# Query projection of a hybrid trunk layer: head groups A and B in three chunks of 512 columns instead of four of 384

## The reference, cut to what matters

```python
z = h @ w_in                                   # h: (384, 2048), w_in: (2048, 3648)
a_q, a_k, a_v, b_q, b_k, b_v, c_q, c_ckv, c_kr = jnp.split(z, PROJ_SPLITS, axis=-1)
q_a = apply_rope(rms_norm(a_q, lp["a_qn"]), *rope_hd)      # latent tiles; context tiles without the rope
q_b = apply_rope(rms_norm(b_q, lp["b_qn"]), *rope_hd)
...                                            # attention of each group
mix = merge_heads(o_a, o_b, o_c) @ w_o
x = x + g1 * mix
x = x + g2 * hier_moe(modulate(rms_norm(x, g_ffn), sh2, sc2))   # 32 experts of 512, top 2
```

## Time and profile before

| | us |
|---|---|
| median of 3 runs | 1730.23 (1730.15 to 1730.38) |
| the profiled execution's own time | 1730.17 |
| its span, first to last instruction | 1728.3 |
| TensorE busy, matmuls | 1619.3 (94% of the span) |
| VectorE / ScalarE / GpSimd busy | 619.3 / 265.4 / 99.0 |
| read from HBM | 584.04 MB |

### The profile page before, as it was taken

One profiled execution on the slowest core, in us unless ns is written; L12 is line 12 of the kernel. 1 busy time (PEld: TensorE's weight loads), 2 busy tenths in 40 slices (PEclk: granted clock), 3 DMA queues, 4 the chain that ended last, 5 costly groups with the idle time before them and its releaser, 6 DMA issues.

```text
span 1728.3 us, 18419 instructions
## 1 busy us (share of the span) xinstructions
PE 1619.3 (94%) x6799; PEld 661.0 (38%) x6844; DVE 619.3 (36%) x1333; ACT 265.4 (15%) x709; POOL 99.0 (6%) x189
## 2 busy tenths in 40 slices
PE   5999999999989999999999999999899989988998
PEld 2445545544433444444323332332333233233332
DVE  3112222102226201352443454444444443544444
ACT  2003221102224100011011101101110110111010
POOL 1022100101011100000000000000000000000000
PEclk8999999999999999999999999999999999999999
DMA  9994671755569722189999999999999999999995
GB/s 369 384 342 195 250 270 62 281 211 205 227 225 374 316 97 97 60 331 425 425 429 427 427 429 426 425 428 424 425 428 425 428 425 427 426 426 427 416 428 223
DMA packets 92639, 581.93 MB, mean 337 GB/s; under 512 B 9110, under 2 KB 24310, under 8 KB 55390
## 3 DMA queue, kind: packets, MB, share of 16 engines
q1 hardware_dynamic: 84944, 554.20, 78.9%
q0 software_dynamic: 5920, 22.61, 3.5%
q10 hardware_dynamic: 1728, 4.51, 0.7%
HBM read 584.04 MB, written 7.05 MB: 342 GB/s over the span
## 4 chain that ended last, share of the span: by engine, by line
PE 71%; DMA 15%; DVE 2%; issue 2%; ACT 1%; SPq 0%; ACTq 0%
PE bank L1226 24%; DMA ring<-in_w 15%; PE bank L974 13%; PE bank L1076 10%; PE bank L1136 7%; PE bank L871 3%; PE bank L1258 2%; PE bank L1061 2%; PE bank L1185 2%; PE bank L1273 1%; PE bank L1208 1%; PE bank L1122 1%; PE bank L1036 1%; PE bank L1044 1%; PE bank L1011 1%
## 5 line engine op out<-in xcount | busy, mean ns | idle before, releaser
L1226 PE MATMUL bank<-ring,r 128*64 128x512 f32 x1920 | 470.6, 620 | 44.1 <-DMA ring<-in_w 44.1
L1226 PEld LDWEIGHTS bank<-ring,r 128*64 128x64 f32 x1920 | 129.6, 140 | 303.0 <-issue 303.0
L974 PE MATMUL bank<-ring,r 128*128 128x384 f32 (+1 forms) x672 | 243.1, 520 | 0.0
L1916 DVE TENSOR_TENSOR bank<-bank,r 128x512 f32<-128x512 f32 x192 | 134.2, 699 | 278.8 <-PE bank L1136 266.1
L1258 PE MATMUL bank<-ring,mod_row 128*64 128x512 f32 x896 | 196.2, 594 | 8.2 <-ACT mod_row L1472 7.9
L1076 PE MATMUL bank<-ring,r 128*128 128x512 f32 x384 | 169.6, 595 | 0.7 <-issue 0.7
L974 PEld LDWEIGHTS bank<-ring,r 128*128 128x128 f32 x672 | 126.9, 191 | 109.8 <-issue 46.5
L1136 PE MATMUL bank<-r 128*128 128x512 bf16 x495 | 137.6, 382 | 7.2 <-issue 7.2
L1918 DVE TENSOR_TENSOR r<-r,bank 128x512 f32<-128x512 f32 x192 | 131.8, 686 | 6.6
L1258 PEld LDWEIGHTS bank<-ring,mod_row 128*64 128x64 f32 x896 | 75.3, 137 | 119.5 <-issue 109.3
L1076 PEld LDWEIGHTS bank<-ring,r 128*128 128x128 f32 x384 | 71.3, 190 | 82.2 <-issue 82.1
(11 more groups left out here) (270 smaller groups left out, 1201.5 us busy)
## 6 DMA issues: line engine op xcount, KB each, us to landing
ring<-in_w SPq DMA_DIRECT2D x180, 2048.0 KB, 17.5
ring<-in_w_mod SPq DMA_DIRECT2D x96, 1024.0 KB, 13.1
ring<-in_w SPq DMA_DIRECT2D x19, 1024.0 KB, 7.5
ring<-in_w_o SPq DMA_DIRECT2D x16, 1024.0 KB, 11.1
ring<-in_w_in SPq DMA_DIRECT2D x20, 768.0 KB, 6.0
ring<-in_w_in SPq DMA_DIRECT2D x8, 1024.0 KB, 5.3
r<-mod_d POOLq DMA_DIRECT2D x8, 1024.0 KB, 16.8
r<-in_w SPq DMA_DIRECT2D x5, 1024.0 KB, 8.4
```

The costliest lines, as they stand in the source:

```text
L974: mm = pe.matmul(acc[acc_of(a)][:, 0:w], h_t[:, k, t * P:(t + 1) * P], wu[:, j, :], start=(k == 0), stop=(k == KD - 1))
L1226: mm = pe.matmul(ps[64 * c:64 * c + 64, :], xg_t[:, j, 64 * c:64 * c + 64], big_cut(slot_of(u), (8, 512))[:, j % 8, :], start=(j == 0), st ...
L1916: v.tensor_tensor(ps[:, :], ps[:, :], g2b[:, min(t, 1), cols], ALU.mult).then_inc(strip_scaled, 1)
```

## The change: what it does

The 1536 query columns of groups A and B are cut in three chunks of four heads (512 columns) in place of four chunks of three heads (384 columns). `q0` is A's heads 0 to 3, `q1` is A's heads 4 and 5 with B's heads 0 and 1, `q2` is B's heads 2 to 5. The columns of `q1` don't lie together, so its four units are each 8 row blocks of 256 columns, from A and from B in turn, and each matmul reads two neighbouring ring slots as one operand of 2 x 256. It starts a half of the chunk only when both of that half's units are there.

```diff
-          ("aq0", Q_A, 384), ("aq1", Q_A + 384, 384), ("bq0", Q_B, 384),
-          ("akv", K_A, 512), ("bq1", Q_B + 384, 384), ("bkv", K_B, 512)]
+          ("q0", Q_A, 512), ("q1", Q_A + 512, 512), ("akv", K_A, 512), ("q2", Q_B + 256, 512),
+          ("bkv", K_B, 512)]
+Q_KINDS = ("q0", "q1", "q2")
...
-RING_FROM = 8
+RING_FROM = 0
...
-            attends = (name == "aq0" and t > 0) or (name == "aq1" and t < 2) or name in ("bq1", "bkv")
+            attends = (name == "q0" and t > 0) or (name == "q1" and t < 2) or name in ("q2", "bkv")
...
-                mods(3 if name == "aq0" or (name, t) == ("bq0", 0) else 2)
+                mods(3 if name in ("q0", "q1", "akv") or (name, t) == ("q2", 0) else 2)
...
-        junk = r3_next(384)
-        rope_tmp = r3_next(4, 192)
+        junk = r3_next(512)
+        rope_tmp = r3_next(4, 128)
...
+                if name == "q1":
+                    at += i % 2 * (Q_B - at)
+                    return ins["w_in"][0].rearrange("(j p) n -> p j n", p=P)[:, 8 * (i // 2):8 * (i // 2) + 8, at:at + 256], (8, 256)
...
+                if s[0] == "proj" and jobs[s[1]][0] == "q1":
+                    frees[done.pop()] = (acc_full, acc_uses)
...
+                    if name == "q1":
+                        for k in range(KD):
+                            m = unit_no[("in", name, k // 8 * 2)]
+                            if k % 8 == 0:
+                                arrived(m)
+                                arrived(m + 1)
+                            at = ring_slot(m)
+                            both = ring[:, at:at + 2, :].rearrange("p s (j n) -> p s j n", j=8)[:, :, k % 8, :]
+                            mm = pe.matmul(acc[acc_of(a)][:, :].rearrange("q (s n) -> q s n", s=2),
+                                           h_t[:, k, t * P:(t + 1) * P], both, start=(k == 0), stop=(k == KD - 1))
+                            if k == KD - 1:
+                                mm.then_inc(acc_full, 1)
+                            elif t == TILES - 1 and k in (7, 8):
+                                mm.then_inc(slot_free[ring_slot(unit_no[("in", name, k - 7)])], 1)
...
-                    if kind in ("aq0", "aq1", "bq0", "bq1", "akv", "bkv"):
-                        heads = 3 if kind[1] == "q" else 2
-                        gn = gain_of[kind[0] + ("_qn" if kind[1] == "q" else "_kn")]
...
                         if jobs[n][1]:
-                            after(last)
-                            last = rope(z[:, 0:heads * HD].rearrange("p (h x) -> p h x", h=heads), heads, 64,
-                                        *tables(jobs[n][1], ("cos", "sin")))
+                            for i in range(0, len(names), 2):
+                                after(last)
+                                last = rope(z[:, i * HD:(i + 2) * HD].rearrange("p (h x) -> p h x", h=2), 2, 64,
+                                            *tables(jobs[n][1], ("cos", "sin")))
```

More of the change, by code:

```diff
@@ L247, in plan @@
             else:
-                mods(3 if name == "aq0" or (name, t) == ("bq0", 0) else 2)
+                mods(3 if name in ("q0", "q1", "akv") or (name, t) == ("q2", 0) else 2)
             if name == "akv" and t == 0:
                 steps.append(("cache", "a"))
-            if name == "aq0" and t:
+            if name == "q0" and t:
                 attend("C", [t - 1])
-            if name == "aq1" and t < 2:
+            if name == "q1" and t < 2:
                 attend("C", [t + 2], flush=(t == 1))
-            if name == "bq1":
+            if name == "q2":
                 if t == 0:
@@ L319, in build @@
     n_pv_c = sum(atts[u][0] == "C" for u in pv_units)
-    pv_bank_from = in_turn.index(jobs.index(("bq1", 0)))
+    pv_bank_from = in_turn.index(jobs.index(("q2", 0)))
     def acc_of(r):
@@ L967, in _ @@
                     acc_wait(a)
+                    if name == "q1":
[12 more added lines that the diff above has]
+                                mm.then_inc(slot_free[ring_slot(unit_no[("in", name, k - 7)])], 1)
+                        a += 1
+                        continue
                     for i in range(4):
@@ L1001, in _ @@
                     pe.wait_ge(norm_ready, n + 1)
-                    if kind in ("aq0", "aq1", "bq0", "bq1"):
-                        cols = [0, P, 2 * P]
+                    if kind in Q_KINDS:
+                        cols = [0, P, 2 * P, 3 * P]
                     elif kind in ("cq0", "cq1"):
@@ L1337, in _ @@
                         e.wait_ge(state_out, 16 * states)
-                    if kind in ("aq0", "aq1", "bq0", "bq1"):
-                        heads, w = 3, HD
+                    if kind in Q_KINDS:
+                        heads, w = 4, HD
                     elif kind in ("cq0", "cq1"):
@@ L1369, in _ @@
                     else:
-                        last = e.activation(z[:, 0:384], ps[:, 0:384], ACT.Copy)
+                        last = e.activation(z[:, 0:heads * w], ps[:, 0:heads * w], ACT.Copy)
                     last.then_inc(z_ready, 1)
@@ L1398, in _ @@
                         last = e.activation(dst, ps[:, 0:256].rearrange("p (h x) -> p h x", h=2), ACT.Copy)
-                    elif kind in ("aq0", "aq1", "bq0", "bq1"):
-                        t = jobs[n][1]
-                        h0 = {"aq0": 0, "aq1": 3, "bq0": 6, "bq1": 9}[kind]
-                        last = e.activation(qo[:, t, h0:h0 + 3, :].rearrange("p h x -> p (h x)"), ps[:, 0:384], ACT.Copy)
+                    elif kind in Q_KINDS:
+                        t, h0 = jobs[n][1], 4 * Q_KINDS.index(kind)
+                        last = e.activation(qo[:, t, h0:h0 + 4, :].rearrange("p h x -> p (h x)"), ps[:, :], ACT.Copy)
                     elif kind in ("cq0", "cq1"):
@@ L1729, in scale_by @@
                                                       op0=ALU.mult, op1=ALU.mult)
-                    if kind in ("aq0", "aq1", "bq0", "bq1", "akv", "bkv"):
-                        heads = 3 if kind[1] == "q" else 2
-                        gn = gain_of[kind[0] + ("_qn" if kind[1] == "q" else "_kn")]
-                        for i in range(heads):
-                            last = scale_by(z[:, i * HD:(i + 1) * HD], z[:, i * HD:(i + 1) * HD], i, gn)
+                    if kind in ("akv", "bkv") + Q_KINDS:
+                        if kind in Q_KINDS:
+                            names = ["a_qn" if 4 * Q_KINDS.index(kind) + i < HEADS_A else "b_qn" for i in range(4)]
+                        else:
+                            names = [kind[0] + "_kn"] * 2
+                        for i, name in enumerate(names):
+                            last = scale_by(z[:, i * HD:(i + 1) * HD], z[:, i * HD:(i + 1) * HD], i, gain_of[name])
                         if jobs[n][1]:
-                            after(last)
-                            last = rope(z[:, 0:heads * HD].rearrange("p (h x) -> p h x", h=heads), heads, 64,
-                                        *tables(jobs[n][1], ("cos", "sin")))
+                            for i in range(0, len(names), 2):
+                                after(last)
+                                last = rope(z[:, i * HD:(i + 2) * HD].rearrange("p (h x) -> p h x", h=2), 2, 64,
+                                            *tables(jobs[n][1], ("cos", "sin")))
                     elif kind in ("cq0", "cq1"):
@@ L2039, in _ @@
                     heads, dim = {"ckv": (1, KV_RANK), "cq0": (2, 192), "cq1": (2, 192), "kvc": (2, 192),
-                                  "akv": (2, HD), "bkv": (2, HD)}.get(kind, (3, HD))
+                                  "akv": (2, HD), "bkv": (2, HD)}.get(kind, (4, HD))
                     sv = ss[b][:, 0:heads]
```

## The result

The changed kernel takes 1733.74 us in the median of 20 runs (1731.35 to 1738.05), beside 1730.16 us (1728.72 to 1731.34, 20 runs) of the kernel before. The ratio is 1.0024, with a 95% interval of 1.0018 to 1.0030. So it is slower by 3.6 us. Its runs scatter over 6.7 us, those of the kernel before over 2.6.

The account below looks back on a forecast made before the run. TensorE was taken to bound the kernel up to the output projection, then the weight stream. Jobs and mods -0.9, wait +3.24, clock +1.85 gave +4.2 on 1730.23: 1734.4 us, ratio 1.0024, range 1731.3 to 1737.3.

Parts of the forecast that it names:

- The relay: Whole program: TensorE sets the time up to the output projection, then the weight stream; earlier changes move the end equally.
- Jobs and mods: Query jobs and modulation steps (mods): fewer, wider jobs gain 0.5 us, regrouped mods 0.4; together -0.9 us.
- The wait: Behind the third akv job, TensorE waits for VectorE's read of group 3, queued behind that job's norm: +3.24 us.
- The clock: First q2 job: the new gap brings a half-speed fall of its own, +1.85 us, bounds nothing and 3.7.
- the falls change places: Rival, 0.24: the gap brings a fall but the one at 407 us goes, clock's net cost nothing; 1732.5 us.
- the clock costs twice: Rival, 0.15: longer fall at the gap, or another in output stage or C attention, +1.85 more; 1736.3 us.
- Late weights: Rival, 0.07: akv's second unit lands late, TensorE stands 3.9 us at twice the usual landing; 1738.3 us.
- the wait that isn't there: Rival, 0.08: VectorE's read early enough or the norm too short to matter, no clock fall; 1729.3 us.

Follow-up runs that it names:

- e1_apart: Changed kernel with one modulation step (mod) moved from the third akv job to the first q2 job; 1729.43 us, ratio 1.0000.
- e9: Kernel before, four 384-column chunks, with mods spread to the places where TensorE waits, two in attention A's last flush; 1724.29 us, ratio 0.9967.
- e8: Changed kernel with two mods behind the third akv job, one each side of its transposes, two in attention A's last flush; 1723.03 us, ratio 0.9960.
- e2: Kernel before, four 384-column chunks, with two mods moved from the second akv job to the third; 1733.62 us, ratio 1.0021.
- e3: Changed kernel with the third akv job's norm moved behind the three mods, so VectorE reads the finished group first; 1732.07 us, ratio 1.0011.
- e0_again: Changed kernel unedited, run again for a second trace; 1736.56 us in the median of 5 runs, ratio 1.0037.
- e11_spread_again: The e8 kernel (changed kernel with mods spread to TensorE's waits) run again on another chip; 1724.0 us in 11 runs, ratio 0.9973.
- e12_flush_only: Changed kernel with only two mods behind q2's first job moved into attention A's last flush, boundary wait left in; 1731.83 us, ratio 1.0015.

## Why the prediction was right, point by point

**The relay** held. The changed kernel's end moved by 1.6 us for a start of the output projection 1.5 us later, and over nine traces, whose stages differ by 15 us, what follows is the same to 0.5. What the prediction left out is a fall of the clock behind the output projection, which moved the end by 1.3 us in the other five.

**Jobs and mods**, -0.9 us. The jobs take 13.73 to 13.84 us, `q1`'s two-slot operand costs nothing (13.73 in the chain against 13.74), three mods 2.69. So the rows say -0.9. The times can't: 0.5 us by e1_apart against before and 0.8 by e9 against e8, each with overlapping runs.

**The wait**, +3.24 us. Measured 3.14, in each trace of the kernel, and in the old chunks too. The norm starts 2.53 us behind the job's end (predicted 2.54), the read at 4.52 (4.54), TensorE goes on 0.83 behind it (0.84). The 0.1 is in the mods and the transposes ahead of the wait: 377.09 - 374.88 = 2.21 us, since the pair is counted to its end (1.90) and not by its pitch (1.83). The cause was settled by moving the mods (e1, e2) and the norm (e3).

**The clock**, +1.85 us. This is the term that was only right in the mean. I had one fall of one size added, and no other changed. No trace shows that. The size was a little high: the slow job at 407.05 took 12.17 us from start to start of what follows, and the one at its place in e9 takes 418.02 - 407.54 = 10.48 at full clock, so the fall cost 1.7 us. The first trace has the gap's fall with the one at 407 us gone (net +0.1), which was the rival "the falls change places": 1732.5 us forecast, 1731.96 measured. The two traces of 1737 us lose 4.5 us more than before, with a longer fall at the gap and one at attention C: the rival "the clock costs twice", 1736.3 forecast, 1737.84 and 1737.15 measured. e0_again fits neither: the gap brought no fall at all. The two groups of runs lie at 1732.7 and 1736.7, and about half of the runs are in each. The forecast of 1734.4, 0.7 us above the median, stands between the groups. So the wait was predicted and the place was right; that the point came out so close owes something to the mean of two cases that were both rivals.

The Trainium skill, "TensorE: Matmul & The Clock Gate", says in the section on what is actually happening that the gate runs free of the kernel. I had set against it that three runs of the kernel before lay within 0.23 us. With more runs the traces agree with the page on this point: equal waits at attention C with and without a fall behind them, and 2.6, 4.9 and 9.3 us lost by one program.

**Late weights** and the wait that isn't there are refuted: no DMA in the waits in any of the four traces of the kernel, and the wait in all four.

**Open.** Why the kernel before keeps to 1727.85 to 1731.39 us in 90 runs, though the flush of attention C can fall in its order too (e9), isn't settled. Nor is it shown what the four long runs of e11_spread_again lost.

## What to carry to other kernels

When a chunk or tile size changes, everything that was dealt out between the pieces shifts with it: look at who has become neighbours, above all where one accumulator's last use and next first use now stand together, and whether the engine that frees it has other work queued ahead. Work without a due time belongs where the matmul engine waits, and mending one such wait can show little until the next is mended too, since the clock may fall at another, as in e12_flush_only. Where the clock falls in and out, one profile names the waits but not the median: take several, and keep what was lost at half speed apart from the rest.

## What the runs showed of the hardware that was not expected

- One program, with waits equal from run to run, lost 2.6, 4.9 or 9.3 us to half speed on TensorE in the stage of the projection and attention. Its runs lie in two groups 4 us apart.
- Three mod steps of 0.95 us put elsewhere (e8: one behind the transposes, two in the flush) left no half-speed stretch in a stage of 371 us in both traces, and brought 10.6 us (1734.1 to 1723.5), of which the rest of the stage accounts for 4.7.
- All nine traces with the last flush of attention A empty, with its wait of 1.99 us, fall to half speed there and lose 1.5 to 3.1 us; none of the five with two mods in it does.
- Filling a gap of 3.1 us with matmuls of no use kept the clock up at that place in the trace, and gave no gain that 7 runs can show (1733.6 against 1734.1 us).
- A matmul whose moving operand is 2 x 256 columns from two neighbouring buffers takes what one of 512 columns takes: 13.73 us against 13.74 for a job of 16.
- Behind the output projection, after waits of 0.41 and 0.69 us, the same eight matmuls took 3.68 us in nine traces and 5.3 to 5.4 in five.
